# Three weight remainders of the first attention, moved from VectorE's quarters to whole GpSimd instructions

## The chip, the cores and the metric

The kernel runs on one core of one Trainium2 chip. The metric is the device time of one execution in microseconds (us), taken as the median of several runs.

## The reference, cut to what matters

A network of three blocks over 256 tokens of width 1024, all in float32. The change lies in the first block's attention (16 heads, 96 features per query and key, 64 per value) and at the product with `w_o` behind it:

```
q = rms_norm(q, g_qn); k = rms_norm(k, g_kn)          # per head, then rope
logits = einsum('bqhd,bkhd->bhqk', qi, k) * scale     # two blocks of 128 queries, causal
probs = softmax(logits)
o = einsum('bhqk,bkhd->bqhd', probs, v)
h = h + o.reshape(b, s, 1024) @ w_o                   # w_o: 1024 x 1024
```

Then comes a feed-forward stage that begins with the rms norm of `h`. All else of the reference is as before in both kernels.

## The kernel before, in words

**Weights.** A float32 product is made of three products of rounded operands: a value is split into a rounded part and the remainder. Weights come in numbered groups of 256 rows x 1024 columns (or 512 x 512), 128 partitions x 2048 elements, through a ring of four slots (`RING`), slot = group mod 4. SyncE loads group n into `raw`; ScalarE rounds it into `wh` (its `split`, or `split_half` for half a group) and counts in `hi_done`; VectorE makes the remainder `wl = raw - wh` (its `split` at L1986, or `split_quarter` at L1994) and counts in `lo_done`. TensorE waits for the count in `lo_done` (`wait_group`), and SyncE waits for the same count before it overwrites `raw` in that slot (`room`).

**First attention.** Its groups are g to g+13; g+10 to g+13 hold `w_o`. Group g+10 is split before the heads. The heads are a hand-written software pipeline of steps i = 6 to 18 behind a hand-written beginning. TensorE's step i is: transposes of head i's queries and keys (L690), scores of head i-1 (L842 to L845), transposes of the probabilities of head i-2 (L690), values of head i-3 (L863). VectorE's step i is: the negated maxima of head i-1's scores (L2313, L2314, from PSUM) and their product with the keys' norm, `nmx` (L2317, both inputs in SBUF); head i's keys out of PSUM into `qkT` (L2305, `copy_keys`); head i-2's turned probabilities into `pT` (L2324) and a reciprocal (L2326); head i-3's output (L2332). ScalarE's step i is: head i's queries into `qkT` (L1682), then head i-1's exponentials, which need `nmx` (L1692). All queues run in order, so that the scores of a head wait for `copy_keys` of that head, which stands on VectorE behind `nmx` of the head before.

**The quarters.** From step 8 on each step of VectorE ends with `split_quarter`, 128x512 elements: twelve of them (the twelfth a second one in step 18), the remainders of groups g+11, g+12, g+13. ScalarE rounds these three groups in halves: g+11 in the beginning, g+12 after steps 6 and 7, g+13 after steps 8 and 9.

**GpSimd** has short work here: the rope products (L2849 to L2852, 128x128 elements) and the inverse roots (L2808, L2809, 128x8 elements) of heads 0 to 7 and then of heads 8 to 15. Behind the last of them its queue waits for the values of head 15 and then issues a load of `p` and nine copies of a bias table (L2862, L2865).

**After the heads** TensorE turns the outputs (`turn_o`) and multiplies by `w_o`: `o_high` (L926, L927) and `o_low` (L934), the latter waiting for `xl` from VectorE's `rest_rows` (L2380), whose first bank stands between the last steps. Then VectorE's `matrix_out` adds the result to `h`.

Of the kernel before, what the change touches and what calls it, by code (L numbers as in the profile page):

```python
# [18 lines left out]
F32 = mybir.dt.float32  # L19
# [3 lines left out]
ALU = mybir.AluOpType  # L23
# [11 lines left out]
H = 16  # L35
# [7 lines left out]
RING = 4  # L43
GC = 2048
# [32 lines left out]
def plan():  # L77


    sizes = {  # L80
        "norm": (0, 0, (1, 1, 1, 1), (4, 4, 4, 4)),
        "ffn": (33, 13, (6, 5, 0, 0), (6, 5, 0, 0)),
        "ffn_t": (33, 13, (6, 5, 0, G3), (6, 5, 0, G3)),
        "ffn_p": (33, 13, (6, 5, 1, 0), (6, 5, 1, 0)),
        "mla": (14, 12 + H, (H // 2 + 2, H // 2 + 2, H + 2, H + 1), (H + 2, H + 2, H + 2, H + 1)),
        "fox": (17, 9, (H, H, H, H + 3), (H, H, H, H + 3)),
        "ple": (5, 4, (0, 0, 0, 0), (0, 0, 0, 0)),
        "b2": (40, 26, tuple([n + 2 * (b == 3) for b, n in enumerate(U_FILLS)]),
               tuple([n + 2 * (b == 3) for b, n in enumerate(U_FILLS)])),
    }  # L90
    order = [("n0", "norm"), ("f0", "ffn_t"), ("n1", "norm"), ("mla", "mla"), ("n2", "norm"),
             ("f1", "ffn_p"), ("n3", "norm"), ("p0", "ple"), ("n4", "norm"), ("f2", "ffn"), ("n5", "norm"),
             ("fox", "fox"), ("n6", "norm"), ("f3", "ffn_p"), ("n7", "norm"), ("p1", "ple"), ("n8", "norm"),
             ("b2", "b2")]
    g = q = 0
    f, r = [0] * 4, [0] * 4
    at = {}
    for name, kind in order:
        at[name] = (g, q, tuple(f), tuple(r))
        dg, dq, df, dr = sizes[kind]  # L100
        g, q = g + dg, q + dq
        f = [a + b for a, b in zip(f, df)]
        r = [a + b for a, b in zip(r, dr)]
    return at, g


PLAN, NGROUPS = plan()
# [43 lines left out]
def build(nc, I, out):  # L151
    with ExitStack() as ctx:
        def sem(name):
            return ctx.enter_context(nc.semaphore(name))
# [4 lines left out]
        def sb(name, shape, dt=F32):  # L159
            n = int(np.prod(shape[1:])) * (2 if dt == BF16 else 4)  # L160
            t = nc.alloc_sbuf_tensor_at(name, list(shape), dt, offset=BASE + top[0])
            top[0] += (n + 31) // 32 * 32
            return t

        BASE = (nc.sbuf_base + 63) // 64 * 64
        raw = sb("raw", [P, RING, GC])
        wh = sb("wh", [P, RING, GC], F32R)
        wl = sb("wl", [P, RING, GC], F32R)
# [163 lines left out]
        hi_done = sem("hi_done")  # L332
        lo_done = sem("lo_done")
# [1631 lines left out]
        def _(dve):  # L1965
            done = [2]
# [19 lines left out]
                dve.tensor_tensor(wl[:, s, 0:n], raw[:, s, 0:n], wh[:, s, 0:n].bitcast(F32), ALU.subtract)\  # L1986
                   .then_inc(lo_done, 1)

            def split_quarter(n):

                g = done[0]
                s, w = g % RING, slice(n * GC // 4, (n + 1) * GC // 4)
                dve.wait_ge(hi_done, g - 1)
                e = dve.tensor_tensor(wl[:, s, w], raw[:, s, w], wh[:, s, w].bitcast(F32), ALU.subtract)  # L1994
                if n == 3:
                    e.then_inc(lo_done, 1)
                    done[0] += 1

            def split_half(n):

                g = done[0]
                s, w = g % RING, slice(n * GC // 2, (n + 1) * GC // 2)
                dve.wait_ge(hi_done, g - 1)
                e = dve.tensor_tensor(wl[:, s, w], raw[:, s, w], wh[:, s, w].bitcast(F32), ALU.subtract)
                if n:
                    e.then_inc(lo_done, 1)
                    done[0] += 1

            def split_to(n):
                for g in range(done[0], min(n, NGROUPS)):  # L2010
                    split(g)
                done[0] = max(done[0], min(n, NGROUPS))
# [28 lines left out]
            def scaled(r, t):  # L2041
                dve.wait_ge(rstd_done, NT * r + t + 1)
                return rstd[:, t:t + 1]
# [146 lines left out]
            g, q, f, r = PLAN["mla"]  # L2190
# [184 lines left out]
            def rest_rows(done, banks):  # L2375

                for b in banks:
                    t = b // 2
                    dve.wait_ge(oh_done, done + b + 1)
                    dve.tensor_tensor(xl[:, b % 2::2, t * P:(t + 1) * P],  # L2380
                                      M[:, b, :].rearrange("p (k n) -> p k n", k=4),
                                      xh[:, b % 2::2, t * P:(t + 1) * P].bitcast(F32), ALU.subtract)\
                       .then_inc(m_read[b], 1)

            def matrix_out(g, q, r, nname):

                residual(q, g + 3, 1.0, 0)
                split_to(g + 6)
                rest(nname, r, 0)
                residual(q, g + 3, 1.0, 1)  # L2390
                split_to(done[0] + 1)
                rest(nname, r, 1)
# [3 lines left out]
            for i in range(6, H + 3):  # L2396
                if i == H + 2:
                    rest_rows(OH["mla"], range(1))
                step(i)

                if i == 6:
                    scale_keys(1, 1)
                elif i == 7:
                    sum_queries(1, 1)
                elif i >= 8:
                    split_quarter((i - 8) % 4)
                if i == H + 2:
                    split_quarter(3)
            rest_rows(OH["mla"], range(1, 4))
            matrix_out(g + 10, q + 10 + H, 2, "n2")  # L2410
            ffn("f1", 2, "n3")

# [48 lines left out]
            g, q, f, r = PLAN["fox"]  # L2461
# [93 lines left out]
            for t in range(NT):  # L2555
                e = dve.scalar_tensor_tensor(fl[:, 0, t, :], M[:, 3, t * H:(t + 1) * H], scaled(5, t), bf[:, :],
                                             ALU.mult, ALU.add)
            e.then_inc(m_read[3], 1)
            for n in range(1, 6):
                m = n - n // 3  # L2560
                for k in range(2):
                    w = fox_group(n) + k
# [26 lines left out]
            g, q, _, _ = PLAN["b2"]  # L2589
# [105 lines left out]
            for c, (what, j) in enumerate(B2_CHUNKS):  # L2695
                fill = q + B2_FILL[c]
                for k in range(2):
                    w = 2 * c + k
# [39 lines left out]
                if c == 12:  # L2738
                    pf = q + B2_YAT
                    for k in range(4):  # L2740
                        if k % 2 == 0:
                            dve.wait_ge(oh_done, OH["b2"] + k + 2)
                        e = dve.scalar_tensor_tensor(yal[:, k, :],
                                                     acc(pf, k // 2)[:, (k % 2) * S:(k % 2 + 1) * S],
                                                     gains[:, G_POOL + k:G_POOL + k + 1],
                                                     yah[:, k, :].bitcast(F32), ALU.mult, ALU.subtract)
# [11 lines left out]
            for t in range(NT):  # L2758
                for n in range(2):
# [6 lines left out]
                    e = dve.tensor_tensor(mg[:, t, cols], mg[:, t, cols], orev[:, n, :], ALU.add)  # L2766
# [30 lines left out]
        def _(pool):  # L2797
# [8 lines left out]
            def inverse_rms(dst, src, n, width, signal):  # L2806

                link(pool.tensor_scalar(dst, src, 1.0 / width, EPS, ALU.mult, ALU.add))  # L2808
                pool.tensor_tensor(dst, dst, mhalf[:, 0:n], ALU.pow).then_inc(signal, 1)  # L2809
# [25 lines left out]
            for c in range(2):  # L2835
                for t in range(NT):
                    pool.wait_ge(heads_ss, 2 * NT * c + t + 1)
                    inverse_rms(hrs[:, 2 + t, 8 * c:8 * c + 8], hss[:, 2 + t, 8 * c:8 * c + 8], 8, DQ, heads_rstd)
                for t in range(NT):
                    for n in (2 * c, 2 * c + 1):  # L2840
                        fill = PLAN["mla"][1] + MLA_Q_FILL[n]
                        pool.wait_ge(acc_read[fill % 2], acc_reads(fill))
                    qv = qn[:, t, :].rearrange("p (h d) -> p h d", d=DQ)[:, 8 * c:8 * c + 8]
                    tb = [tab[:, 0, t, j, :].unsqueeze(1).to_broadcast([P, 8, 16]) for j in range(4)]
                    x1, x2 = qv[:, :, NOPE:NOPE + 16], qv[:, :, NOPE + 16:DQ]
                    pool.wait_ge(heads_sq, 2 * NT * c + NT + t + 1)
                    m4 = [rt[:, 2 * t + m // 2, 8 * (m % 2):8 * (m % 2) + 8, :] for m in range(4)]
                    for m, (x, j) in enumerate(((x1, 0), (x2, 1), (x1, 2), (x2, 3))):
                        e = pool.tensor_tensor(m4[m], x, tb[j], ALU.mult)  # L2849
                    link(e)  # L2850
                    pool.tensor_tensor(x1, m4[0], m4[1], ALU.subtract)
                    e = pool.tensor_tensor(x2, m4[2], m4[3], ALU.add)  # L2852
                    if t:
                        e.then_inc(q_rotated, 1)
                    else:
                        link(e)
                for t in range(NT):
                    pool.wait_ge(heads_ss, 2 * NT * c + NT + t + 1)
                    inverse_rms(hrs[:, t, 8 * c:8 * c + 8], hss[:, t, 8 * c:8 * c + 8], 8, DQ, heads_rstd)
            pool.wait_ge(m_ready[3], PLAN["n2"][2][3])  # L2860
            pool.wait_ge(table_out, 16)
            pool.dma_start(p_n[:, :, :], I["p"][0, 0].rearrange("(t p) n -> p t n", p=P)).then_inc(p_in, 16)  # L2862
# [153 lines left out]
```

## Time and profile before

| | before |
|---|---|
| median of 3 runs | 1336.75 us (1336.58 to 1338.41) |
| the profiled execution's own time | 1337.19 us |
| its span, first to last instruction | 1335.4 us |
| mean granted TensorE clock | 0.998 of full speed |
| TensorE matmuls busy | 1316.5 us, 99% of the span |
| VectorE busy | 798.0 us, 60% |
| ScalarE busy | 679.4 us, 51% |
| GpSimd busy | 128.8 us, 10% |

All times in rows are from the start of the span. The first attention's heads take the stretch from 249 to 294 us. A row of the timeline has an instruction's start and duration; neighbours on one engine overlap by some 0.08 us, so that the distance of two starts is what an instruction costs its queue.

### The profile page before, as it was taken

The page shows a single profiled execution, that of the slowest core. Times are in us where ns is not written, and L with a number is a line of the kernel's source. Part 1 is how long each engine was busy: PE and PEld are TensorE (multiplying, and loading weights), DVE is VectorE, ACT ScalarE, POOL GpSimd, SP SyncE. Part 2 cuts the span into 40 slices and gives each one's busy share as a digit, 9 for nine tenths or more (in the row PEclk, how much of TensorE's full clock was granted, in tenths as well). Part 3 has the DMA queues.
Part 4 walks back from the last instruction along what each step waited for, and adds up shares of the span by engine and source line. Part 5 has one row for each costly group of instructions (what it writes and reads, how often), then busy time and mean ns, then how long its engine had stood idle before and what let it go on. Part 6 is the DMA issues. An engine that isn't in the chain of part 4 may idle for free.

```text
span 1335.4 us, 17481 instructions
## 1 busy us (share of the span) xinstructions
PE 1316.5 (99%) x6474; PEld 1078.3 (81%) x6474; DVE 798.0 (60%) x1036; ACT 679.4 (51%) x959; POOL 128.8 (10%) x199
## 2 busy tenths in 40 slices
PE   8999999999999999999999999999999999999997
PEld 6888788788888887888888777888888877788886
DVE  6755448885555546655544667655554655665674
ACT  6444427755444426644444557544443646457542
POOL 2000002712000000000000330100000042110000
PEclk9999999999999999999999999999999999999999
DMA  9665544336655654555553654466564397555441
GB/s 299 219 188 189 189 154 165 98 95 190 204 182 184 218 194 144 180 186 187 180 204 126 227 183 127 134 188 188 188 220 160 128 266 246 167 163 172 160 158 32
DMA packets 148782, 236.46 MB, mean 177 GB/s; under 512 B 10087, under 2 KB 103447, under 8 KB 148208
## 3 DMA queue, kind: packets, MB, share of 16 engines
q1 hardware_dynamic: 143600, 222.26, 51.1%
q0 software_dynamic: 4736, 12.96, 3.3%
q8 instruction: 40, 0.66, 0.2%
q10 hardware_dynamic: 384, 0.41, 0.1%
q14 instruction: 22, 0.18, 0.0%
HBM read 233.43 MB, written 4.51 MB: 178 GB/s over the span
## 4 chain that ended last, share of the span: by engine, by line
PE 88%; DVE 5%; ACT 3%; issue 2%; DMA 1%; POOL 0%; SPq 0%; POOLq 0%; DVEq 0%; ACTq 0%
PE acc L614 19%; PE acc L616 19%; PE acc L615 19%; PE acc L647 7%; PE acc L648 7%; PE acc L651 7%; PE misc L690 5%; DVE wl L1986 2%; ACT wh L1461 1%; PE misc L1270 1%; DMA raw<-in_ffn_w_in_dram 1%; PE misc L1127 1%; ACT xh L1505 0%; DVE pT L2324 0%; ACT hn L1493 0%
## 5 line engine op out<-in xcount | busy, mean ns | idle before, releaser
L1986 DVE TENSOR_TENSOR wl<-raw,wh 128x2048 fp32r<-128x2048 f32 (+2 forms) x201 | 453.2, 2261 | 266.0 <-ACT wh L1461 265.9
L1461 ACT ACTIVATE wh<-raw 128x2048 fp32r<-128x2048 f32 (+2 forms) x207 | 388.7, 1888 | 138.8 <-PE acc L651 124.7
L614 PE MATMUL acc<-wh,xh 128*128 128x512 f32 (+1 forms) x832 | 329.0, 395 | 2.8 <-DVE xl L2030 1.3
L616 PE MATMUL acc<-wh,xl 128*128 128x512 f32 (+1 forms) x832 | 323.2, 388 | 0.0
L615 PE MATMUL acc<-wl,xh 128*128 128x512 f32 (+1 forms) x832 | 322.6, 388 | 0.0
L614 PEld LDWEIGHTS acc<-wh,xh 128*128 128x128 f32 x832 | 156.3, 188 | 36.9 <-DVE wl L1979 4.4
L616 PEld LDWEIGHTS acc<-wh,xl 128*128 128x128 f32 x832 | 156.2, 188 | 32.8
L615 PEld LDWEIGHTS acc<-wl,xh 128*128 128x128 f32 x832 | 156.5, 188 | 30.1
L647 PE MATMUL acc<-wh,ah 128*128 128x512 f32 x320 | 125.7, 393 | 0.0
L648 PE MATMUL acc<-wl,ah 128*128 128x512 f32 x320 | 124.6, 389 | 0.0
L614 PE MATMUL acc<-wh,zh 128*128 128x512 f32 x272 | 108.5, 399 | 1.5 <-DVE wl L1986 1.0
L616 PE MATMUL acc<-wh,zl 128*128 128x512 f32 x272 | 106.2, 390 | 0.0
L615 PE MATMUL acc<-wl,zh 128*128 128x512 f32 x272 | 106.0, 390 | 0.0
L1550 ACT ACTIVATE ah<-misc 128x512 f32 (+1 forms) x44 | 26.4, 599 | 156.0 <-PE misc L690 156.0
L651 PE MATMUL acc<-wh,al 128*128 128x512 f32 x320 | 98.5, 389 | 0.0
L2808 POOL TENSOR_SCALAR rstd<-ssq 128x1 f32<-128x1 f32 x19 | 9.4, 493 | 924.4 <-ACT hn L1493 924.4
L1544 ACT ACTIVATE sg<-acc,rstd 128x256 f32<-128x256 f32 x88 | 41.4, 475 | 100.5 <-PE acc L616 100.5
L2146 DVE TENSOR_TENSOR al<-misc,ah 128x512 f32 (+1 forms) x44 | 30.4, 692 | 84.0 <-ACT ah L1550 84.0
L1505 ACT ACTIVATE xh<-misc,gains 128x128 fp32r<-128x128 f32 x128 | 40.4, 364 | 68.8 <-PE misc L690 59.7
L647 PEld LDWEIGHTS acc<-wh,ah 128*128 128x128 f32 x320 | 60.1, 188 | 13.8 <-issue 1.7
L651 PEld LDWEIGHTS acc<-wh,al 128*128 128x128 f32 x320 | 60.1, 188 | 12.6
L648 PEld LDWEIGHTS acc<-wl,ah 128*128 128x128 f32 x320 | 60.1, 188 | 12.2
(363 smaller groups left out, 1654.1 us busy)
## 6 DMA issues: line engine op xcount, KB each, us to landing
raw<-in_ffn_w_in_dram SPq DMA_DIRECT2D x172, 512.0 KB, 4.7
raw<-in_ffn_w_out_dram SPq DMA_DIRECT2D x88, 512.0 KB, 4.4
raw<-in_w_in_dram SPq DMA_DIRECT2D x64, 512.0 KB, 4.8
raw<-in_fox_w_in_dram SPq DMA_DIRECT2D x24, 512.0 KB, 4.4
raw<-in_ple_w_gate_dram SPq DMA_DIRECT2D x16, 512.0 KB, 4.1
raw<-in_mla_w_o_dram SPq DMA_DIRECT2D x8, 512.0 KB, 4.1
raw<-in_fox_w_o_dram SPq DMA_DIRECT2D x8, 512.0 KB, 4.5
raw<-in_w_out_dram SPq DMA_DIRECT2D x8, 512.0 KB, 4.4
```

The source lines that it names most:

```text
L614: pe.matmul(dst, hi, rhs_h, start=first, stop=False)
L615: pe.matmul(dst, hi, rhs_l, start=False, stop=False)
L616: return pe.matmul(dst, lo, rhs_h, start=False, stop=last)
L647: pe.matmul(acc(q + n, t), xa, wh[:, s, r], start=st, stop=False)
L648: pe.matmul(acc(q + n, t), xa, wl[:, s, r], start=False, stop=False)
L651: mm = pe.matmul(acc(q + n, t), xb, wh[:, s, r], start=False, stop=en)
L690: return pe.transpose(M[0:rows, b, cols], src, m[:, :])
L1461: act.activation(wh[:, s, 0:n], raw[:, s, 0:n], ACT.Copy).then_inc(hi_done, 1)
L1505: act.activation(x_cols(xh, r, k, t), turned(r, k, t), ACT.Copy, scale=gains[:, c:c + 1]).then_inc(xh_done, 1)
L1544: act.activation(sg[:, c % 2, t, :], acc(q, t)[:, 0:256], ACT.Silu, scale=rstd[:, t:t + 1]).then_inc(silu_done, 1)
L1986: dve.tensor_tensor(wl[:, s, 0:n], raw[:, s, 0:n], wh[:, s, 0:n].bitcast(F32), ALU.subtract)\
L2146: dve.tensor_tensor(al[:, bass.ds(i * 4 + 2 * c, 2), :], pair(M[:, b, :]), ah[:, bass.ds(i * 4 + 2 * c, 2), :].bitcast(F32), ALU.subtract)\
```

## The change

The eleven steps 8 to 18 lose their quarters on VectorE, and the twelfth goes too. GpSimd gets three `tensor_tensor` subtractions of a whole group each, 128x2048 elements, behind its last inverse root and ahead of its loads. Each waits for ScalarE's rounding of its group (`hi_done`) and for the remainder of the group before (`lo_done`), so that the count keeps its order. VectorE waits for the three before it goes on behind the heads.

```
@@ VectorE
-            def split_quarter(n):
-
-                g = done[0]
-                s, w = g % RING, slice(n * GC // 4, (n + 1) * GC // 4)
-                dve.wait_ge(hi_done, g - 1)
-                e = dve.tensor_tensor(wl[:, s, w], raw[:, s, w], wh[:, s, w].bitcast(F32), ALU.subtract)
-                if n == 3:
-                    e.then_inc(lo_done, 1)
-                    done[0] += 1
...
                 elif i == 7:
                     sum_queries(1, 1)
-                elif i >= 8:
-                    split_quarter((i - 8) % 4)
-                if i == H + 2:
-                    split_quarter(3)
             rest_rows(OH["mla"], range(1, 4))
+
+            dve.wait_ge(lo_done, g + 12)
+            done[0] = g + 14
             matrix_out(g + 10, q + 10 + H, 2, "n2")
@@ GpSimd, behind the inverse roots of heads 8 to 15
+            g = PLAN["mla"][0]
+            for n in range(g + 11, g + 14):
+                pool.wait_ge(hi_done, n - 1)
+                pool.wait_ge(lo_done, n - 2)
+                pool.tensor_tensor(wl[:, n % RING, :], raw[:, n % RING, :], wh[:, n % RING, :].bitcast(F32),
+                                   ALU.subtract).then_inc(lo_done, 1)
             pool.wait_ge(m_ready[3], PLAN["n2"][2][3])
```

VectorE's queue in a middle step of the heads, before:

```order
L2317 TENSOR_TENSOR nmx<-mxp,hrs 128x2
L2305 TENSOR_SCALAR qkT<-misc,headg 96x256
L2324 COPY pT<-misc 128x384
L2326 RECIPROCAL rin<-rs 128x2
L2332 TENSOR_TENSOR hn<-misc,rin 128x2x64
L1994 TENSOR_TENSOR wl<-raw,wh 128x512
```

and now:

```order
L2307 TENSOR_TENSOR nmx<-mxp,hrs 128x2
L2295 TENSOR_SCALAR qkT<-misc,headg 96x256
L2314 COPY pT<-misc 128x384
L2316 RECIPROCAL rin<-rs 128x2
L2322 TENSOR_TENSOR hn<-misc,rin 128x2x64
```

The quarter at the step's end is gone; the rest keeps its order, with line numbers ten lower.

GpSimd's queue behind the rope products of heads 8 to 15 (`heads_ss` counts VectorE's sums of squares, `p_step` is GpSimd's own), before:

```order
L2808 TENSOR_SCALAR hrs<-hss 128x8 [waits heads_ss]
L2809 TENSOR_TENSOR hrs<-hrs,mhalf 128x8 [waits p_step]
L2862 DMA p_n<-in_p_dram 128x2x256 [waits table_out,m_ready3]
L2865 DMA bias_by_offset<-bias_table 8x64x128 x9
```

and now:

```order
L2797 TENSOR_SCALAR hrs<-hss 128x8 [waits heads_ss]
L2798 TENSOR_TENSOR hrs<-hrs,mhalf 128x8 [waits p_step]
L2854 TENSOR_TENSOR wl<-raw,wh 128x2048 [waits lo_done,hi_done] x3
L2858 DMA p_n<-in_p_dram 128x2x256 [waits table_out,m_ready3]
L2861 DMA bias_by_offset<-bias_table 8x64x128 x9
```

The three subtractions stand directly behind the last inverse root. TensorE's, ScalarE's and SyncE's queues are the same in both kernels.

## Rows read from the trace of the kernel before

**Rows 1.** The page, busy time by engine.

```profile
PE 1316.5 (99%) x6474; PEld 1078.3 (81%) x6474; DVE 798.0 (60%) x1036; ACT 679.4 (51%) x959; POOL 128.8 (10%) x199
```

**Rows 2.** TensorE's waits: waited for, us in total, times, longest.

```profile
PE acc L842 <- DVE qkT L2305: 2.8, 5, 1.1
```

**Rows 3.** Timeline, VectorE, steps 9 to 17: start, us, engine, line, operation [idle before].

```profile
272.58 0.16 DVE L2317 TENSOR_TENSOR nmx<-mxp,hrs 128x2 f32<-128x2 f32 x1
...
276.44 0.68 DVE L1994 TENSOR_TENSOR wl<-raw,wh 128x512 fp32r<-128x512 f32 x1
277.04 0.28 DVE L2313 TENSOR_REDUCE mxp<-acc 128x1 f32<-128x128 f32 x1
...
277.69 0.16 DVE L2317 TENSOR_TENSOR nmx<-mxp,hrs 128x2 f32<-128x2 f32 x1
277.80 0.48 DVE L2305 TENSOR_SCALAR qkT<-misc,headg 96x256 f32<-96x256 f32 x1
...
290.09 0.17 DVE L2317 TENSOR_TENSOR nmx<-mxp,hrs 128x2 f32<-128x2 f32 x1
```

**Rows 4.** Timeline, TensorE, one step: scores, end of scores, next transposes, next scores.

```profile
275.85 0.49 PE L842 MATMUL acc<-qkT 96*128 96x128 f32 x2
...
276.72 0.22 PE L845 MATMUL acc<-causal,identb 128*128 128x128 bf16 x1
...
277.95 0.38 PE L690 MATMUL misc<-ident,kn 128*96 128x128 f32 x2
278.33 0.38 PE L842 MATMUL acc<-qkT 96*128 96x128 f32 x1
```

**Rows 5.** Timeline, TensorE and VectorE at the end of the heads.

```profile
293.43 0.78 PE L863 MATMUL misc<-vn,pT 128*128 128x64 f32 x6
294.19 0.73 PE L934 MATMUL acc<-wh,xl 128*128 128x512 f32 x2
...
293.45 0.68 DVE L2380 TENSOR_TENSOR xl<-misc,xh 128x512 fp32r<-128x512 f32 x1
```

**Rows 6.** Timeline, GpSimd, where the three subtractions will stand.

```profile
269.62 0.20 POOL L2808 TENSOR_SCALAR hrs<-hss 128x8 f32<-128x8 f32 x1 [3.86 <-DVE hss L2237]
269.90 1.65 POOL L2809 TENSOR_TENSOR hrs<-hrs,mhalf 128x8 f32<-128x8 f32 x1
297.59 0.82 POOL L2862 DMA_DIRECT2D p_n<-in_p_dram  x1 [26.04 <-PE misc L690]
```

**Rows 7.** Timeline: a rope product of GpSimd and VectorE's remainder that began before it.

```profile
240.37 1.76 DVE L1986 TENSOR_TENSOR wl<-raw,wh 128x1536 fp32r<-128x1536 f32 x1 [0.24 <-ACT wh L1461]
...
240.45 2.01 POOL L2849 TENSOR_TENSOR rt<-qn,tab 128x128 f32<-128x128 f32 x1
```

**Rows 8.** Timeline: `nmx` behind a rope product that began before it.

```profile
260.58 0.46 POOL L2849 TENSOR_TENSOR rt<-qn,tab 128x128 f32<-128x128 f32 x1
...
260.68 0.38 DVE L2317 TENSOR_TENSOR nmx<-mxp,hrs 128x2 f32<-128x2 f32 x1
```

**Rows 9.** Timeline: `nmx` beside an inverse root, the output beside a rope product.

```profile
264.11 1.65 POOL L2809 TENSOR_TENSOR hrs<-hrs,mhalf 128x8 f32<-128x8 f32 x1
...
264.54 0.16 DVE L2317 TENSOR_TENSOR nmx<-mxp,hrs 128x2 f32<-128x2 f32 x1
...
257.81 0.27 DVE L2332 TENSOR_TENSOR hn<-misc,rin 128x128 f32<-128x128 f32 x1
```

**Rows 10.** Timeline, ScalarE: second halves of the rounding of g+12 and g+13.

```profile
268.55 1.05 ACT L1469 ACTIVATE wh<-raw 128x1024 fp32r<-128x1024 f32 x1
...
273.77 1.05 ACT L1469 ACTIVATE wh<-raw 128x1024 fp32r<-128x1024 f32 x1
```

**Rows 11.** Stretches (engines' busy time, then granted clock PEclk), and TensorE's last matmul.

```profile
263.00:265.20 2.20, 1.11 (x12) 0.86 (x10) 2.17 (x7) 0.95 (x5) 2.03 (x3) 1.00 0.00 0
1328.00:1331.00 3.00, 0.00 (x0) 0.00 (x0) 1.13 (x2) 1.37 (x3) 0.82 (x2) 0.78 0.00 0
...
1327.30 0.39 PE L616 MATMUL acc<-wh,zl 128*128 128x512 f32 x1
```

## The prediction

> **What bounds the kernel now.** I read first the busy times: TensorE is busy for 99% of the span [rows 1], so whatever can be won is a piece of its few waits, and whatever delays it goes to the end nearly whole. The waits say where the heads stand: TensorE's scores waited for VectorE's keys, 2.8 us in all [rows 2]. So I read the heads' timeline on VectorE and TensorE. The pattern repeats every 2.48 us: from step 11's `nmx` at 277.69 to the last at 290.09 it is 12.40 us for five heads [rows 3]. In the same step TensorE's scores begin at 275.85 and the next at 278.33, also 2.48 us [rows 4].
>
> Who sets this pace? VectorE has no gap: its quarter starts at 276.44 and the maxima follow at 277.04, 0.60 us later [rows 3]. But that isn't all that stands in the ring. The scores start at 275.85 and their last matmul ends at 276.72 + 0.22 = 276.94 [rows 4]; the maxima could have begun about 0.05 us later (an estimate: the distance of the other handover, from the keys' end to the scores), at 276.99. From the maxima to the end of the keys' copy it is 277.04 to 277.80 + 0.48 = 278.28, and the next scores start at 278.33 [rows 3, 4]. This ring of dependences, scores, maxima, `nmx`, keys, scores, is 1.14 + 1.24 + 0.05 = 2.43 us long without any quarter in it. VectorE's queue with the quarter is 2.48 us. TensorE's own work in a step is 2.32 us: its last transposes take the queue from 277.95 to 278.17, and it waits 0.16 us for the keys until 278.33 [rows 4].
>
> **What the change takes away.** VectorE loses eleven times 0.60 us and one more quarter, 7.2 us of its time. Of this only what lies between the queue's 2.48 and the ring's 2.43 us comes off the path: 0.05 us in a head. The other 0.55 us becomes idle time of VectorE at the end of each step. At the end of the heads there is a second gain: `o_low` starts at 294.19 behind `xl`, which started at 293.45 and took 0.68, while TensorE was through with the values at 293.43 + 0.62 = 294.05 [rows 5]. Without the quarter before it `xl` is ready 0.60 us sooner, and 0.14 us goes. The most that the change can bring is so 8 x 0.05 + 0.14, about 0.5 us.
>
> **What it adds.** Three subtractions of 128x2048 elements on GpSimd. No row has one. The nearest is the rope product, 128x128 elements in 0.46 us [rows 8], and a small instruction takes 0.20 us for 128x8 [rows 6]. If 0.19 us of each is fixed, an element costs 0.27/128 us, and 2048 of them 4.3 us: 4.5 us together. The bounds: with nothing fixed 16 x 0.46 = 7.4 us; from below VectorE's own 1.76 us for 1536 elements, 2.3 us for 2048 [rows 7]. I take 4.5 us, nearest to GpSimd's own rows, where the two shapes show that a fixed part exists. The Trainium skill (GPSIMD Engine Reference, "Elementwise — side-by-side cycle accounting") gives 4497 ns for an addition of this size and type; by it the sum would be the same.
>
> **When they run.** The last inverse root starts at 269.90 and takes 1.65 us [rows 6]; 0.08 us behind it the first subtraction starts, at 271.63. Its rounding is done before the others', that of g+12 is done at 269.6, that of g+13 at 274.8 [rows 10], or some 3.5 us later if ScalarE is held up, which is still before its turn. So the three follow one another and end near 285.4, far before TensorE needs the last of these groups (behind `o_low`'s 294.19, rows 5) and before GpSimd's loads at 297.59 [rows 6]. The added wait of VectorE behind the heads finds the count reached, costs nothing, and SyncE's loads of the next groups are released earlier than now.
>
> **What they run beside.** This is the term that decides. In two places the trace has GpSimd and VectorE both reading two tensors in SBUF. A rope product that began 0.08 us after VectorE's remainder took 2.01 us in place of 0.46, to 242.46; the remainder ran to 242.13, and since neighbours overlap by 0.08 us the product came 0.41 us behind its place in the queue [rows 7]. It stood still for the whole of VectorE's instruction. And the reverse: `nmx` at 260.68, behind a rope product of 260.58, took 0.38 us in place of 0.16 and ended at 261.06, when the product was through at 261.04 [rows 3, 8]. VectorE's instructions with one input in PSUM are not touched (the output at 257.81 took its 0.27 us beside a product) [rows 9]. The new subtraction has two inputs in SBUF and lasts 4.5 us; `nmx` has two inputs in SBUF, is in the ring, and comes in every step. So each subtraction holds up the `nmx` that comes while it runs, until it ends.
>
> One row speaks for less: beside an inverse root of 1.65 us `nmx` took its 0.16 us [rows 9]. That instruction reads 8 elements in a partition and is slow for another reason; I take it that the way is shut while GpSimd reads, and a subtraction reads until near its end.
> The Trainium skill (SBUF — State Buffer, "Who interferes with whom") says that a VectorE instruction with two SBUF inputs and a GpSimd instruction that reads SBUF exclude each other, the later one waiting for the whole of the earlier. Rows 7 and 8 agree; the inverse root of rows 9 would by it have held `nmx` to 265.76, and did not. For the sum both readings give the same.
>
> **The sum.** The first `nmx` to meet a subtraction is the one of 272.58 (0.05 earlier now): held to 271.63 + 4.5 = 276.13, 3.6 us. It then takes 0.12 us, and the second subtraction starts. The next `nmx` is due 2.43 us after the last one, at 278.6, and is held to 280.75, 2.2 us; the third likewise to 271.63 + 3 x 4.5 + 2 x 0.12 = 285.37. That `nmx` is the one that stood at 277.69 [rows 3]: +7.68 us. Then the subtractions are over; five heads to the last `nmx` win 5 x 0.05 = 0.25, and the tail 0.14. Together +7.29 us. TensorE has no slack behind the heads to take this up. On the profiled execution: 1337.19 + 7.29 = 1344.5 us; the median of the runs lies 0.44 us under that execution, so 1344.0 us.
>
> **Rivals.**
> *The way is not shut for long* (not slower): GpSimd reads a long operand in pieces, or its reads run ahead as in the inverse root [rows 9], so that `nmx` slips through. Then only the gain of 0.5 us is left: 1336.2 us. At the lower bound of 2.3 us for a subtraction the first would cost 1.4 us and the later ones, shorter than a head, nothing: 1337.6. With T for the time that each subtraction shuts the way the sum above is 3T - 6.21; it reaches 2.7 us, which a measurement can tell, at T = 3.0 us: below that the kernel is not slower. Against it: the 0.38 us of rows 8, a wait for nearly the whole of the product. 10%.
> *TensorE's clock.* At the program's end the last matmul is over at 1327.69, and over the 3 us from 1328 the granted clock is 0.78, the lower level (1.2 GHz) for some 44% of them, so it fell about 2.0 us after TensorE went still; the 1.09 us wait within 263 to 265.2 left it at 1.00 [rows 11]. The first stall leaves TensorE still for 3.4 us, so the clock may well fall. Most of that costs nothing: even at twice 2.32 = 4.64 us a step fits into the 4.62 us from one subtraction to the next. If it is still low behind the third, each head costs 4.64 in place of 2.43 us: +2.2, two of them +4.4, 1346.2 to 1348.4 us. 9%.
> *GpSimd goes first.* If the next subtraction wins over the waiting `nmx`, the first two hold it to 280.7; the third's rounding waits behind this `nmx` (exponentials, then half a rounding, 2.1 us), and holds the next one to about 287.3 against 277.69 - 2.48 = 275.21 now. That is 12.1 less about 0.4 of gains, 11.7 us, 1348.4 us. Against it: in rows 8 `nmx` got in although the next product stood ready. 4%.
> *A dearer subtraction*, up to 7.4 us each: 3 x 7.4 - 6.21 = +16.0 us, 1352.7 us. 3%.
>
> **How the numbers follow.** Forecast 74%; its own ends are 4 us (+5.8, 1342.5) and 5 us (+8.8, 1345.5) for a subtraction. The range goes from 1341.0, which leaves room for a way that opens a little before the end of each subtraction, to 1348.5, which holds the clock's case and GpSimd's first turn; left out are the open way and the dear subtraction. A measurement of this kernel can tell 0.2%, 2.7 us, from no change. Slower by more than this: forecast, clock, first turn, dear one, 90%, less 1 for mixtures: 89%. Within it: the open way, 10%. Faster by more than 2.7 us would need more than the whole gain of 0.5: 1%.
>
> **What would show it.** Three GpSimd instructions of about 4.5 us from 271.6 to 285.4; three `nmx` of about 3.6, 2.3 and 2.3 us in place of 0.16, each ending with one of them, and the other thirteen at 0.16; TensorE's waits for `qkT` up from 2.8 to near 10 us; after them a pace of 2.43 us in a head, VectorE idle about 0.5 us in each; `o_low` without a wait. Wrong would be: `nmx` at 0.16 us beside a subtraction, a subtraction that grows because VectorE shuts it out, or a lower granted clock behind 285 us.

## The result, and the profile after

The changed kernel takes 1344.37 us (median of 4 runs, 1344.14 to 1346.52), beside 1336.74 us before (4 runs, 1336.58 to 1338.41): 7.63 us slower, a ratio of 1.0058 with a 95% interval of 1.0045 to 1.0070. The profiled execution of the changed kernel took 1344.35 us, with a span of 1342.5 us. The mean granted clock was 0.994 to 0.995 in all four executions of the changed kernel, beside 0.998 in the profiled execution before.

The page's busy times and TensorE's waits in the changed kernel, the counterparts of [rows 1] and [rows 2] (L2295 is the keys' copy, L2305 before):

```profile
PE 1319.1 (98%) x6474; PEld 1081.2 (81%) x6474; DVE 798.2 (59%) x1024; ACT 679.1 (51%) x959; POOL 142.3 (11%) x202
```

```profile
PE acc L842 <- DVE qkT L2295: 7.5, 7, 3.3
```

GpSimd is busy for 13.5 us more. VectorE's busy time didn't fall although it lost twelve quarters: instructions that stand still count as busy. TensorE waits 7.5 us for the keys in place of 2.8. That is less than the "near 10 us" of the prediction: the first hold shows in it with 3.3 us, the second with only 1.4 and the third with nothing, because TensorE's own work took longer at the lower clock (below) and filled the time.

The timeline of GpSimd, counterpart of [rows 6]; the last row is the first subtraction alone:

```profile
269.02 1.64 POOL L2798 TENSOR_TENSOR hrs<-hrs,mhalf 128x8 f32<-128x8 f32 x1
270.63 13.83 POOL L2854 TENSOR_TENSOR wl<-raw,wh 128x2048 fp32r<-128x2048 f32 x3
...
270.63 4.51 POOL L2854 TENSOR_TENSOR wl<-raw,wh 128x2048 fp32r<-128x2048 f32 x1
```

And VectorE's in the same stretch, counterpart of [rows 3]: `nmx` of six heads and of the last one, and one copy of keys.

```profile
271.64 3.51 DVE L2307 TENSOR_TENSOR nmx<-mxp,hrs 128x2 f32<-128x2 f32 x1
275.08 0.47 DVE L2295 TENSOR_SCALAR qkT<-misc,headg 96x256 f32<-96x256 f32 x1
...
277.39 2.43 DVE L2307 TENSOR_TENSOR nmx<-mxp,hrs 128x2 f32<-128x2 f32 x1
...
282.93 1.55 DVE L2307 TENSOR_TENSOR nmx<-mxp,hrs 128x2 f32<-128x2 f32 x1
...
287.59 0.16 DVE L2307 TENSOR_TENSOR nmx<-mxp,hrs 128x2 f32<-128x2 f32 x1
...
290.09 0.16 DVE L2307 TENSOR_TENSOR nmx<-mxp,hrs 128x2 f32<-128x2 f32 x1
292.51 0.17 DVE L2307 TENSOR_TENSOR nmx<-mxp,hrs 128x2 f32<-128x2 f32 x1
...
297.38 0.17 DVE L2307 TENSOR_TENSOR nmx<-mxp,hrs 128x2 f32<-128x2 f32 x1
```

The first subtraction ends at 270.63 + 4.51 = 275.14 and the held `nmx` at 271.64 + 3.51 = 275.15; the third ends at 284.46 and the third `nmx` at 284.48. Three `nmx` are held, each to the end of one subtraction. But the third became due only at 282.93, 5.54 us after the second had; and from the keys' copy at 284.40 it took 3.30 us to the next one at 287.70, not 2.43. The stretches say why: TensorE's clock (columns: stretch, its length, busy times, granted clock, DMA).

```profile
272.00:274.00 2.00, 0.34 (x4) 0.09 (x1) 2.00 (x1) 0.00 (x0) 2.00 (x1) 1.00 0.00 0
276.00:278.00 2.00, 2.00 (x15) 1.85 (x14) 1.51 (x6) 1.59 (x4) 2.00 (x1) 0.78 0.79 225
278.00:280.00 2.00, 0.85 (x4) 0.41 (x2) 2.00 (x2) 0.14 (x1) 1.86 (x2) 0.50 0.85 299
284.00:286.00 2.00, 1.98 (x9) 1.47 (x8) 1.59 (x5) 1.45 (x5) 0.46 (x1) 0.50 0.42 113
286.00:288.00 2.00, 2.00 (x13) 1.63 (x13) 1.04 (x4) 0.21 (x1) 0.00 (x0) 0.66 0.95 278
288.00:290.00 2.00, 2.00 (x20) 1.84 (x18) 1.47 (x6) 1.24 (x5) 0.00 (x0) 1.00 0.65 228
```

TensorE stood still from 272.3 to 275.6, worked again, and then went to the lower level (0.50, 1.2 GHz): 0.78 over the 2 us from 276 means from about 277.1, 0.66 from 286 means until about 287.4.

**The account.** From the first `nmx` that is held to the last of the stage it is 271.64 to 297.38 = 25.74 us now, and was 272.58 to 290.09 = 17.51 us [rows 3]: +8.23. From there to `o_low` it is 3.91 us (301.29 in the trace) and was 4.10 [rows 3, 5]: -0.19. The last root stands 0.88 us earlier in this execution than in the one before (269.02 and 269.90 [rows 6]), in a part that the change leaves alone, and `nmx` another 0.06. 8.23 - 0.19 - 0.88 - 0.06 = 7.10 us, which is the difference of the spans.

### The profile page after: what moved, and what is told of

The parts are those of the page before. It is cut to its first block, busy times and chain, and to the rows that moved or that the text cites. A ratio compares the mean times of both kernels' runs of the same rounds, so it can differ in the third digit from the quotient of the medians.

```text
span 1342.5 us, 17476 instructions
## 1 busy us (share of the span) xinstructions
PE 1319.1 (98%) x6474; PEld 1081.2 (81%) x6474; DVE 798.2 (59%) x1024; ACT 679.1 (51%) x959; POOL 142.3 (11%) x202
## 3 DMA queue, kind: packets, MB, share of 16 engines
HBM read 233.43 MB, written 4.51 MB: 177 GB/s over the span
## 4 chain that ended last, share of the span: by engine, by line
PE 89%; DVE 5%; ACT 3%; issue 2%; POOL 0%; DMA 0%; POOLq 0%; SPq 0%; DVEq 0%; ACTq 0%
PE acc L614 20%; PE acc L616 19%; PE acc L615 19%; PE acc L647 7%; PE acc L651 7%; PE acc L648 7%; PE misc L690 5%; DVE wl L1986 2%; ACT wh L1461 1%; PE misc L1270 1%; PE misc L1127 1%; PE acc L844 1%; ACT xh L1505 0%; PE misc L863 0%; PE acc L842 0%
```

## The experiments

Three theories are to be told apart. **Shut way:** a GpSimd instruction that reads SBUF and a VectorE instruction with two tensor inputs there exclude each other. **Bandwidth:** the loss goes by what GpSimd reads. **Something else of the change:** the added wait, the loads released earlier, the order. Beside them the question what TensorE's clock cost, and whether the remainders could be moved with a gain.

| run | median us | ratio to before, 95% |
|---|---|---|
| e1_tiny | 1336.17 | 0.9997 (0.9988 to 1.0006) |
| e2_halves | 1339.49 | 1.0028 (1.0019 to 1.0037) |
| e3_quarters | 1336.65 | 1.0000 (0.9991 to 1.0009) |
| e4_memset | 1336.03 | 0.9995 (0.9986 to 1.0004) |
| e5_scalars | 1337.50 | 1.0006 (0.9997 to 1.0015) |
| e6_act_after | 1337.67 | 1.0008 (0.9999 to 1.0017) |
| e7_act_before | 1338.08 | 1.0009 (1.0000 to 1.0018) |
| e8_filled | 1343.88 | 1.0055 (1.0041 to 1.0069) |
| e9_keys_first | 1344.38 | 1.0055 (1.0042 to 1.0069) |
| e10_before_keys_first | 1342.78 | 1.0044 (1.0030 to 1.0058) |
| e11_quarters_keys_first | 1344.46 | 1.0056 (1.0042 to 1.0069) |
| e12_one_engine | 1336.99 | 1.0001 (0.9992 to 1.0010) |

Before took 1336.61 to 1336.74 us beside them. An interval that holds 1 means no difference that these medians can tell; differences under about 1 us are read from the traces.

### Is it GpSimd's reading? e1_tiny and e4_memset

```
-                pool.tensor_tensor(wl[:, n % RING, :], raw[:, n % RING, :], wh[:, n % RING, :].bitcast(F32),
+                pool.tensor_tensor(wl[:, n % RING, 0:8], raw[:, n % RING, 0:8], wh[:, n % RING, 0:8].bitcast(F32),
                                    ALU.subtract).then_inc(lo_done, 1)
```

> The changed kernel, with 8 of 2048 columns in each of GpSimd's three subtractions; the remainders of the other columns of these three groups are left out. Theory 'shut way' (a GpSimd instruction that reads SBUF and a VectorE instruction with two SBUF inputs exclude each other for as long as GpSimd reads): every nmx back at 0.16 us, only the gain is left, 2.43 us in a head in place of 2.48: about 0.5 us under the kernel before, 1336.2 us. Rival 'the rest of the change costs' (the added wait behind the heads, earlier loads, the missing quarters): it stays above 1338 us.

```
-                pool.tensor_tensor(wl[:, n % RING, :], raw[:, n % RING, :], ..., ALU.subtract).then_inc(lo_done, 1)
+                pool.memset(wl[:, n % RING, :].bitcast(F32), 0.0).then_inc(lo_done, 1)
```

> The three subtractions replaced by three memsets of the same 128x2048 elements (the remainders of these groups are left out: they become zero). GpSimd only writes SBUF. 'Shut way' with the reads as the shared part: nmx stays at 0.16 us beside them, about 1336.2 us. Rival 'any long GpSimd instruction holds VectorE': memsets of about 2 us (0.53 us for 512 columns in the trace before) hold at least the first nmx by over 1 us, 1337.3 us or more.

Both came out as the shut way has it, 1336.17 and 1336.03 us. So nothing else of the change costs anything that these runs can tell. The gain of 0.5 us in the sum is of the size of the noise here (the intervals of both runs hold 1) and is read from the pace: in e1_tiny's timeline the last five heads show the open pace, (289.40 - 277.24) / 5 = 2.43 us:

```profile
277.24 0.17 DVE L2307 TENSOR_TENSOR nmx<-mxp,hrs 128x2 f32<-128x2 f32 x1
...
289.40 0.16 DVE L2307 TENSOR_TENSOR nmx<-mxp,hrs 128x2 f32<-128x2 f32 x1
```

In e4_memset GpSimd writes the same area for 5.65 us, in three instructions of about 1.8 us. An `nmx` falls into the first of them with 0.77 us to go and takes its 0.16 us. (The one at 274.89 says little: the second memset had 0.06 us left.) So a GpSimd instruction that only writes did not hold `nmx`; that the length of one alone does not hold VectorE is shown by e5_scalars below:

```profile
271.23 1.81 POOL L2854 MEMSET wl<- 128x2048 f32 x1
...
271.23 5.65 POOL L2854 MEMSET wl<- 128x2048 f32 x3
...
272.27 0.16 DVE L2307 TENSOR_TENSOR nmx<-mxp,hrs 128x2 f32<-128x2 f32 x1
...
273.15 1.80 POOL L2854 MEMSET wl<- 128x2048 f32 x1
...
274.89 0.16 DVE L2307 TENSOR_TENSOR nmx<-mxp,hrs 128x2 f32<-128x2 f32 x1
```

### The same reading, cut: e2_halves and e3_quarters

```
-                pool.tensor_tensor(wl[:, n % RING, :], raw[:, n % RING, :], ..., ALU.subtract).then_inc(lo_done, 1)
+                for m in range(2):                                # 4 in e3_quarters
+                    w = slice(m * GC // 2, (m + 1) * GC // 2)     # GC // 4
+                    e = pool.tensor_tensor(wl[:, n % RING, w], raw[:, n % RING, w], ..., ALU.subtract)
+                e.then_inc(lo_done, 1)
```

> The same work on GpSimd, each subtraction cut in two of 128x1024. 'Shut way': 0.19 + 4.32 / 2 = 2.35 us each; an nmx waits for the half that runs and slips in between two. Behind a held nmx the next half starts after 0.14 us and ends 2.49 us later, the next nmx is due 2.31 us later: held 0.2 us, six times; the first one 1.3 us. In all + 1.3 + 1.2 - 0.5 = + 2.0 us over the kernel before, 1338.7 us, and the clock stays up. Rival 'bandwidth' (the loss goes by the amount that GpSimd reads, however cut): 1344 us as with whole groups.

> The same work, each subtraction cut in four of 128x512, 0.19 + 1.08 = 1.27 us each. 'Shut way': two of them end 2.68 us behind a held nmx, the next is due at 2.31: held some 0.3 us, six times, the first up to 1.2: + 1.8 + 0.6 - 0.5, about 1338.6 us. 'Bandwidth': 1344 us or more.

Bandwidth falls: GpSimd reads as much in both (14.26 and 15.16 us in all), and the time falls from 1344.4 to 1339.5 and 1336.65 us. The quarters cost less than I expected, 1336.65 and not 1338.6 us: of six `nmx` in the stretch the longest hold was 0.25 us. Two quarters of 1.27 us are nearly as long as a head's 2.43 us, so that they stay about in step with it; the six `nmx` came 2.54 us apart on average. The rows of e3_quarters:

```profile
272.14 0.28 DVE L2307 TENSOR_TENSOR nmx<-mxp,hrs 128x2 f32<-128x2 f32 x1
...
277.30 0.22 DVE L2307 TENSOR_TENSOR nmx<-mxp,hrs 128x2 f32<-128x2 f32 x1
...
282.21 0.41 DVE L2307 TENSOR_TENSOR nmx<-mxp,hrs 128x2 f32<-128x2 f32 x1
```

The halves were 2.35 us long, as expected, and their `nmx` did not keep step. After the first hold (1.36 us) the next `nmx` came at 275.79, 0.06 us before its half's end, and behind ScalarE's half rounding the one after that was due at 278.45, when the next half had run for 0.14 us:

```profile
275.79 0.16 DVE L2307 TENSOR_TENSOR nmx<-mxp,hrs 128x2 f32<-128x2 f32 x1
...
278.45 2.22 DVE L2307 TENSOR_TENSOR nmx<-mxp,hrs 128x2 f32<-128x2 f32 x1
...
278.31 2.34 POOL L2856 TENSOR_TENSOR wl<-raw,wh 128x1024 fp32r<-128x1024 f32 x1
```

With a length near the head's it is chance whether a half is missed by little or met in full. This kernel's 11 executions fall in two kinds: eight of 1339.1 to 1341.0 us with a mean granted clock of 0.998 to 0.999, and three of 1342.5 to 1345.5 us with 0.993 to 0.995. The profiled one, 1344.40 us, is of the three; its clock was 0.50 from about 281.2 to 291.4, for 6 us after GpSimd was through at 285.4. There TensorE's own work set the pace, 4.43 us from scores to scores:

```profile
285.91 0.80 PE L842 MATMUL acc<-qkT 96*128 96x128 f32 x2 [0.18 <-DVE qkT L2295]
...
290.34 0.63 PE L842 MATMUL acc<-qkT 96*128 96x128 f32 x2
```

From the end of the last held `nmx` (285.46) the next two came after 3.11 and 3.98 us, where it is 2.23 and 2.43 us with the clock up (e8_filled, below): 2.4 us lost. This execution lies 4.9 us above the median. The other 2.5 us fit a chain that only this trace shows from one side: at the lower clock the `nmx` of 283.75 came some 0.9 us late, missed the end of the fifth half and was held through most of the sixth, which began at 283.1. No execution of the faster kind was profiled, so that this half of the account is an estimate.

### Is it the second tensor input? e5_scalars

```
-                    dve.tensor_tensor(nmx[:, :, j], mx, hrs[:, 0:NT, j], ALU.mult).then_inc(max_done, 1)
+                    for t in range(NT):
+                        e = dve.tensor_scalar(nmx[:, t, j:j + 1], mx[:, t:t + 1], hrs[:, t, j:j + 1], None, ALU.mult)
+                    e.then_inc(max_done, 1)
```

> The changed kernel with nmx made by two instructions on VectorE, each with one tensor input and the norm as a scalar read by pointer from SBUF, in place of one with two tensor inputs. GpSimd's three whole subtractions stay at 4.5 us. 'Shut way' by the second tensor input: neither is held, each about 0.16 us; the ring is one small instruction longer in all 16 heads, 2.43 + 0.1 us, so 1336.7 + 0.8 = 1337.5 us. Rival 'a pointer scalar from SBUF is shut out as well': they are held as nmx is now, 1345 us.

1337.50 us, as expected. GpSimd's three whole subtractions run from 271.04 for 13.86 us, and `nmx` passes beside them in two instructions, 0.33 us together:

```profile
271.04 13.86 POOL L2856 TENSOR_TENSOR wl<-raw,wh 128x2048 fp32r<-128x2048 f32 x3
...
274.85 0.34 DVE L2308 TENSOR_SCALAR nmx<-mxp,hrs 128x1 f32<-128x1 f32 x2
277.41 0.33 DVE L2308 TENSOR_SCALAR nmx<-mxp,hrs 128x1 f32<-128x1 f32 x2
279.97 0.34 DVE L2308 TENSOR_SCALAR nmx<-mxp,hrs 128x1 f32<-128x1 f32 x2
```

The same values are read from SBUF, the norm as a scalar by pointer and no longer as a second tensor. A head of the steady stretch now takes 2.56 us, 0.13 more, which eats the gain.

### What did the clock cost? e8_filled

```
                     if i < H:
                         turned(i)
+                    if i in (10, 11, 12):
+                        ...
+                        for _ in range(12 if i == 10 else 8):
+                            pe.matmul(acc(sq + i - 1, 1), wh[:, s, 0:P], wh[:, s, 0:512], start=True, stop=True)
                     if 0 <= i - 1 < H:
                         scores(i - 1)
```

> The changed kernel with 12, 8 and 8 extra matmuls (products nobody reads, 0.23 us each) in TensorE's three waits during GpSimd's subtractions, so that TensorE is never still for more than 1 us. Theory 'the clock fell because TensorE was still, and costs only behind the third subtraction': granted clock 1.00 all through, the held nmx are the same three, the fourth nmx comes 2.43 us behind the third and not 3.3: 0.9 us less than the changed kernel, 1343.5 us. Rival 'the clock costs nothing': 1344.4 us.

The granted clock is 1.00 in all stretches from 268 to 296 of the profiled execution. Two of them, where it was at the lower level in the changed kernel:

```profile
276.00:280.00 4.00, 3.75 (x24) 2.93 (x23) 3.51 (x5) 1.68 (x5) 3.86 (x2) 1.00 0.84 261
280.00:284.00 4.00, 3.84 (x26) 3.43 (x27) 3.51 (x7) 1.21 (x5) 4.00 (x1) 1.00 0.72 226
```

`nmx` of three heads is held as before, and the third is now due in step:

```profile
271.40 3.58 DVE L2312 TENSOR_TENSOR nmx<-mxp,hrs 128x2 f32<-128x2 f32 x1
277.22 2.49 DVE L2312 TENSOR_TENSOR nmx<-mxp,hrs 128x2 f32<-128x2 f32 x1
281.94 2.48 DVE L2312 TENSOR_TENSOR nmx<-mxp,hrs 128x2 f32<-128x2 f32 x1
286.65 0.16 DVE L2312 TENSOR_TENSOR nmx<-mxp,hrs 128x2 f32<-128x2 f32 x1
...
296.38 0.16 DVE L2312 TENSOR_TENSOR nmx<-mxp,hrs 128x2 f32<-128x2 f32 x1
```

First held to last: 271.40 to 296.38 = 24.98 us, 0.76 less than the 25.74 of the changed kernel and 7.47 more than before. But the three subtractions took 4.57 to 4.58 us in this execution and 4.51 to 4.52 in the changed kernel's, which hides 0.18 us of the clock's share. From the end of the third held `nmx` to the last `nmx` it is 284.42 to 296.38 = 11.96 us here and 284.48 to 297.38 = 12.90 us in the changed kernel: 0.94 us is what the clock cost. The executions agree: the four with a mean granted clock of 0.998 or 0.999 took 1343.29 to 1343.89 us, the fifth, at 0.995, took 1344.48, and the changed kernel's four, at 0.994 and 0.995, took 1344.14 to 1346.52; the intervals of the two ratios overlap all the same. TensorE ran at the lower level for 10 us, and it cost 0.94, since most of it lay under a held `nmx`.

### Can the remainders be moved with a gain? e6, e7, e9 to e12

e6_act_after and e7_act_before let ScalarE make `nmx`, on the changed kernel and on the kernel before:

```
-                    dve.tensor_tensor(nmx[:, :, j], mx, hrs[:, 0:NT, j], ALU.mult).then_inc(max_done, 1)
...
+                    for t in range(NT):
+                        act.activation(nmx[:, t, j:j + 1], mxp[:, j % 2, t:t + 1], ACT.Copy,
+                                       scale=hrs[:, t, j:j + 1]).then_inc(a_step, 1)
```

> The changed kernel with nmx made by ScalarE (two copies with a scale, 128x1, ahead of the exponentials), so that VectorE has no instruction with two SBUF inputs in the ring. 'Shut way': GpSimd's subtractions run beside the heads and hold nobody; the ring is scores, maxima, keys: 2.43 less about 0.15, at TensorE's own 2.3 us; some 0.15 us less in each head than 2.43: 1336.7 - 0.5 - 2 = 1334.5 us. Rival: ScalarE's four small instructions more make the exponentials late (probabilities wait), no better than 1336.7 us. If something else than nmx is held: 1344 us.

> The kernel before (quarters on VectorE, nothing on GpSimd) with nmx made by ScalarE. VectorE's queue loses 0.11 us and a wait on itself in each step: 2.48 to 2.37 or a little less in the steps with a quarter, about 1.5 us in all, 1335.3 us; it shows what of the former run comes from moving the remainders and what from nmx alone.

Both missed: 1337.67 and 1338.08 us, a little slower than before. Nothing is held any more (GpSimd's whole subtractions take 13.87 us beside the heads and the time is 6.7 us better than the changed kernel's), but ScalarE's queue is now in the way: the exponentials start 0.6 to 0.9 us behind their maxima's end, where it was 0.23, through two small instructions and ScalarE's wait for them. While ScalarE also rounds halves, the queries' copy comes late behind them, the keys' copy waits for it, and a head takes 2.6 to 2.9 us; after that the maxima are 2.19 to 2.57 us apart, 2.38 us on average, so the ring did get shorter, too late to pay. e7_act_before shows the same queue on ScalarE and the same wait for two small instructions. e6_act_after's waits in the heads:

```profile
PE misc L691 <- ACT probs L1699: 1.7, 4, 0.8
PE acc L843 <- DVE qkT L2302: 1.6, 5, 0.3
```

e9 to e11 put the keys' copy ahead of the maxima, to open the ring (e9 on e5_scalars, e10 on the kernel before, e11 on e3_quarters):

```
+                    if i < H:
+                        copy_keys(i)
                     if 0 <= i - 1 < H:
                         maxima(i - 1)
-                    if i < H:
-                        copy_keys(i)
```

> GpSimd's three whole subtractions, nmx by two instructions with a pointer scalar (which were not held), and in VectorE's step the keys' copy of head i ahead of the maxima of head i-1. The keys no longer wait for the maxima, so the ring of 2.43 us is open; then TensorE's own work sets the pace, 2.48 - 0.16 - 0.1 = about 2.22 us in a head (no wait before the scores), and VectorE needs 1.9. Steps 8 to 15: 2.22 in place of 2.48: 1336.7 - 0.5 - 8 x 0.21 = 1334.5 us. Rival 'another ring is as long' (maxima, exponentials, probabilities): about 1336 us.

> The kernel before with nothing but the same two changing places. VectorE's queue with its quarter stays 2.48 us long in steps 8 to 16, so nothing is won: 1336.7 us. If the queue were not the limit it would fall below 1335.5 us. Against the former run it shows what moving the remainders is worth once the ring is open: about 2 us.

> GpSimd's subtractions in quarters of 128x512 with nmx as before (two SBUF inputs), and the keys' copy ahead of the maxima. nmx waits for the quarter that runs, 1.26 us at most, some 0.5 us on average, which VectorE has to spare (2.22 - 1.88 = 0.34 us) only in part: 1335.5 us, between the two others. If holds cost nothing now: 1334.5 us.

All three were wrong by 6 to 10 us. The ring was not opened but closed in another way. The keys' copy waits for ScalarE's copy of the queries from the same PSUM bank, that copy stands on ScalarE behind the exponentials of the head before last, and these wait for `nmx`, which now stands behind the keys' copy. e9_keys_first's timeline on ScalarE and VectorE:

```profile
283.81 0.46 ACT L1692 ACTIVATE probs<-acc,nmx,hrs 128x128 f32<-128x128 f32 x1 [1.55 <-DVE nmx L2308]
...
284.80 0.46 ACT L1682 ACTIVATE qkT<-misc,headg 96x256 f32<-96x256 f32 x1
...
282.80 0.28 DVE L2303 TENSOR_REDUCE mxp<-acc 128x1 f32<-128x128 f32 x1
...
285.40 0.48 DVE L2295 TENSOR_SCALAR qkT<-misc,headg 96x256 f32<-96x256 f32 x1 [0.90 <-ACT qkT L1682]
285.80 0.28 DVE L2303 TENSOR_REDUCE mxp<-acc 128x1 f32<-128x128 f32 x1
```

Maxima, `nmx`, exponentials, queries' copy, keys' copy, maxima: 285.80 - 282.80 = 3.00 us in a head (2.84 in e10_before_keys_first). In the old order this detour is not in the ring, because the maxima do not wait for the keys.

e12_one_engine takes ScalarE's copy out of that ring:

```
 copy_keys(i) on VectorE:
+                    if i >= 7:
+                        dve.tensor_scalar(qkT[0:DQ, i % 2, 0:S], M[0:DQ, tb, 0:S],
+                                          headg[0:DQ, 0:1], None, ALU.mult).then_inc(m_read[tb], 1)
+                    else:
+                        dve.wait_ge(m_read[tb], r[tb] + 2 * tn + 1)
 copy_queries(i) on ScalarE:
+                    if i >= 7:
+                        return
```

> As e9_keys_first (whole subtractions on GpSimd, nmx by two instructions with a pointer scalar, the keys' copy ahead of the maxima), and from head 7 on VectorE copies the queries too, so that the keys' copy no longer waits for ScalarE, whose copy stood behind the exponentials in the ring of e9_keys_first (2.85 to 3.0 us). VectorE's step is then 1.88 + 0.06 + 0.40 = 2.34 us, TensorE's 2.22: 2.34 in place of 2.48 in some nine heads, 1336.7 - 9 x 0.14 - 0.14 = 1335.3 us, and nothing is held by GpSimd. Rival 'maxima, exponentials, probabilities are as long a ring': TensorE waits for probs and the time stays at 1336.2 us or above.

`nmx` of two heads in the timeline, and TensorE's wait in the heads:

```profile
277.97 0.33 DVE L2314 TENSOR_SCALAR nmx<-mxp,hrs 128x1 f32<-128x1 f32 x2
...
280.38 0.33 DVE L2314 TENSOR_SCALAR nmx<-mxp,hrs 128x1 f32<-128x1 f32 x2
```

```profile
PE misc L690 <- ACT probs L1694: 3.0, 4, 0.9
```

7.4 us less than e9_keys_first, which confirms that ring. The pace is 2.41 us, VectorE's own queue; the forecast of 2.34 counted too little for `nmx`, whose two instructions cost the queue 0.25 us and not 0.17. TensorE waits 3.0 us for probabilities, 2.7 of them in three steps before that (265 to 272), while ScalarE rounds. At 1336.99 us it is no faster than the kernel before (ratio 1.0001). No version that beats both kernels clear of noise was found; the kernel before stands beside e3_quarters, and what this idea could bring at most in the old order is e1_tiny's 0.5 us, which its median can't tell from nothing.

## Why the prediction was right

Forecast 1344.0 us in 1341.0 to 1348.5, measured 1344.37. The mechanism is right; that the number is met to 0.4 us is partly luck (last point).

- **The path.** The ring of 2.43 us and its 0.05 us in a head: 2.43 us in e1_tiny and behind the clock's return in the changed kernel. The gain of 0.5 us: 0.55 in e1_tiny's medians, within their noise. `o_low` won 0.19 us where 0.14 was forecast.
- **The price of a subtraction.** 4.5 us forecast from two shapes of GpSimd, 4.51 measured; 2.35 and 1.27 us for the halves and quarters lie on the same line. The Trainium skill's 4497 ns (GPSIMD Engine Reference, "Elementwise — side-by-side cycle accounting") agrees within 0.02 us.
- **The shut way.** Shown by e1_tiny, e4_memset and e5_scalars: it takes a GpSimd instruction that reads and a VectorE instruction with two tensor inputs in SBUF, and either alone is harmless. From the first held `nmx` to the last one the sum was 7.68 - 0.25 = 7.43 us; with the clock kept up (e8_filled) it is 7.47, of which 0.18 is due to that execution's longer subtractions.
- **The clock.** This rival, at 9%, came true in its first half, and with it one of the prediction's own signs of being wrong, a lower granted clock behind 285 us. The sum has no term for it. It was priced at 2.2 us a head, one or two of them, if low behind the third subtraction. It was low there for 2.9 us and cost 0.94. The price holds for a head that lies wholly at the lower level: in e2_halves TensorE's step was 4.43 us there, near the 4.64 of the prediction. In the changed kernel no head did. The first behind the third subtraction still went by the ring, in which only the scores are stretched, and took 3.30 us; then the clock was back. Nor did it fall where [rows 11] led one to look: 2.0 us after TensorE went still would have been 274.3, and it was 1.00 until 276 at least.
- **GpSimd goes first**, 4%: not seen. After each subtraction the waiting `nmx` ended 0.01 us later and the next subtraction started 0.14 us behind the last. **A dearer subtraction:** excluded.
- **What luck did.** On the profiled executions the forecast was +7.29 us and the measured difference is +7.16. The clock's 0.94 us is missing in the sum; the heads' earlier start, 0.88 us in a part that the change leaves alone, took nearly all of it back, and 0.19 us is spread over small terms. Of the thirteen `nmx` that were to stay at 0.16 us one took 0.38, as it did before [rows 8].

What stays open: by what exactly the way is shut. The inverse root of [rows 9] reads 8 elements, runs 1.65 us and held nobody; that the way is free as soon as GpSimd's reads are over fits that row and all runs, but no run varied it.

## What to carry to other kernels

Before moving work to GpSimd, list VectorE's instructions with two tensor inputs in SBUF that will run beside it, and ask which of them stands in a ring of dependences: each will be held for what is left of one GpSimd instruction, so what counts is the length of one such instruction and not their sum. Cut to about half the ring's period (1.27 us beside 2.43 here), or with the second input as a pointer scalar, the same work cost 0.0 and 0.8 us over the kernel before, less than the medians can tell from nothing. Before reordering a queue to open a ring, follow every wait of the moved instruction through the other engines: it may be the one that closes a longer ring.

## What the hardware showed that was not expected

- A pointer scalar read from SBUF didn't count as a second input: `tensor_scalar` took 0.33 us for two beside a subtraction of 4.5 us, and alone.
- A GpSimd memset of 128x2048 float32 takes 1.8 us and did not hold the one `nmx` that fell well inside it.
- TensorE's clock fell not while the engine stood still (272.3 to 275.6) but at about 277.1, 1.5 us after it had begun again, and came back at 287.4, after 10 us in which TensorE was busy for most of the time.
- One and the same kernel (e2_halves) showed a lower mean clock (0.993 to 0.995) in 3 of 11 executions, 3 to 6 us above the median, and 0.998 or 0.999 in the other 8. In the profiled one of the three it fell after two waits of 1.1 and 2.0 us.
